# Five regrouped matmuls in place of six for each 128x128 weight tile, in a two-layer trunk on one Trainium2 core

## The chip, the cores and the metric

The kernel runs as one program on one core of a Trainium2 chip. A core has TensorE (PE; its weight loads are shown apart as PEld), VectorE (DVE), ScalarE (ACT), GpSimd (POOL) and SyncE (SP, which issues most DMAs here). The metric is the device time of one execution in microseconds (us): 2583.07 us, the median of three runs (2578.85 to 2583.41).

## The reference

One step of a two-layer model, on a prompt of 512 tokens and 8 samples of one token each. All of it is float32.

```python
for li in range(DEPTH):                                   # DEPTH = 2
    x = x + 0.5 * swiglu(rmsnorm(x, g_ffa), w_gu, w_down)  # 1024 -> 2 x 2816 -> 1024
    if li == 0: m, ... = ab_mixer(rmsnorm(x, g_mix), ...)  # attention + gated delta rule, with a key and value cache
    else:       m, ... = ret_mixer(rmsnorm(x, g_mix), ...) # retention
    x = x + m
    x = x + 0.5 * swiglu(rmsnorm(x, g_ffb), w_gu, w_down)

def swiglu(x, w_gu, w_down):
    a, b = jnp.split(x @ w_gu, 2, axis=-1)
    return (jax.nn.silu(a) * b) @ w_down
```

The attention of the samples (`fox_sample`) also multiplies each sample's query with 2048 cached keys of each of 4 heads: the samples' key scores.

## The kernel before, in words

The 520 tokens (512 + 8) stand in the free dimension, the features in the 128 partitions: X is 8 chunks of 128 features by 520 tokens. Every large product is done the same way. A float32 activation is held as two float32r tiles, high part and rest (XH and XL before a layer, HH and HL inside a feed-forward part, MOH/MOL and RMOH/RMOL behind the mixers), and so is each weight (WHI, WLO). Of the four partial products three are computed: high x high, rest x high weight, high x rest weight. Since a tile of the result has 520 columns and one bank of PSUM holds 512, the tokens are cut into two halves of 260 in two banks (`ACC[acc][:, n, 0:HALF]`). So each 128x128 weight tile costs 3 x 2 = 6 matmuls of 260 columns, and each of these loads its weights anew. That is `project` (L807).

A *unit* is one column block of weights: 8 weight tiles (contraction 1024), or 11 in the down projection, where two units make one tile of the result. For each unit SP loads RAW, POOL makes WHI (L713) and WLO (L716) of it, and PE multiplies; RAW, WHI and WLO have two slots, so POOL starts on unit u+2 when PE is done with unit u (semaphore `used`). The units stand in this order: up0 (44 units), down0 (16), ab_in (29, the first mixer's input projection: one gate unit and 28), ab_out (8), up1, down1, up2, down2, ret_in (48, the second mixer's input), ret_out (16), up3, down3.

The results are taken out by DVE. In `up` a pair of units gives TA (L1815) and TB (L1818), each multiplied by RSTD; ACT applies Silu to TA (L1416), DVE multiplies (TH, L1822), ACT copies TH to HH (L1418), DVE writes HL (L1824). Four accumulators are used in turn. In up0 and down0 the same ACT queue also issues the loads of LF (L1398), four or five behind each step. In `down` DVE adds the result to X (L1799), ACT squares X (SQ) and writes XH, DVE adds SQ to SSQ (L1782) and writes XL (L1784); PE starts on the next `up` chunk by chunk as XL comes. Two accumulators alternate there, as in ab_in.

In ab_in DVE takes each tile out to PRJ (`take`, L1871) and between two takes computes the samples' key scores (`key_scores`, L1882): 32 batches of 16 products of 128 columns, one or two batches behind each of the last 24 takes. The keys come by DMA into KPAGES. Before that stands a serial part on DVE: the gate unit (L1910) and what is computed from it, with the first four takes in between.

The retention's input (ret_in) calls `project` too.

## Time and profile before

| what | us |
|---|---|
| three runs, median (lowest, highest) | 2583.07 (2578.85, 2583.41) |
| span of the profiled execution | 2571.9 |
| so around the span (load and end of the program), by the median | 11.2 |
| PE busy | 2477.0 (96%) |
| DVE, ACT, POOL busy | 1270.5, 565.3, 1680.7 |

The profiled execution has no time of its own beside its span; the median less the span is taken for what lies around it. A line of the page's last sections reads: line, engine, operation, out<-in, shape, count | busy us, mean ns of one | idle us before, and who ended it. A duration of one matmul is longer than the distance from its start to the next one's start, since matmuls are pipelined; so the distance is worked out from a stretch and its count.

### The profile page before, as it was taken

How to read it: one execution, taken by the hardware profiler on the slowest of the kernel's cores; microseconds unless marked ns; L12 is line 12 of the kernel's file. 1: busy time of each engine (PE TensorE's matmuls, PEld its weight loads, DVE VectorE, ACT ScalarE, POOL GpSimd, SP SyncE). 2: the span in 40 equal slices, each digit the busy share in tenths (PEclk: the TensorE clock that was granted, in tenths of full speed). 3: DMA queues.
4: the chain of work that ended last, by engine and by line, in shares of the span. 5: the costliest groups of instructions: out<-in, count | busy, mean ns of one | idle time of the engine just before them, and what ended most of it. 6: DMA issues, size and time to landing. Idle time of an engine off the chain costs nothing.

```text
span 2571.9 us, 52956 instructions
## 1 busy us (share of the span) xinstructions
PE 2477.0 (96%) x20047; PEld 2384.1 (93%) x20047; DVE 1270.5 (49%) x2226; ACT 565.3 (22%) x848; POOL 1680.7 (65%) x750
## 2 busy tenths in 40 slices
PE   7999998998799899999999999999999899999997
PEld 7999998997577899999999999999999799999996
DVE  4444335787533654443344443367767644444433
ACT  3222101004733222220022220012222211222101
POOL 5777775664413477777777777765555367777773
PEclk9999999998899899999999999999999999999998
DMA  4333333895465333333323333233433333333331
GB/s 121 96 93 91 99 90 85 276 317 175 123 213 185 98 88 93 90 96 90 116 83 90 91 95 101 81 93 113 123 101 109 111 90 90 90 91 92 99 95 56
DMA packets 472391, 291.20 MB, mean 113 GB/s; under 512 B 32785, under 2 KB 438411, under 8 KB 472270
## 3 DMA queue, kind: packets, MB, share of 16 engines
q1 hardware_dynamic: 407286, 221.15, 29.6%
q10 hardware_dynamic: 64992, 68.54, 8.4%
q8 instruction: 72, 1.18, 0.2%
q14 instruction: 41, 0.34, 0.0%
HBM read 273.50 MB, written 16.23 MB: 113 GB/s over the span
## 4 chain that ended last, share of the span: by engine, by line
PE 86%; DVE 7%; ACT 3%; POOL 1%; issue 1%; ACTq 1%; DMA 0%; SPq 0%; DVEq 0%; POOLq 0%
PE ACC L807 76%; PE ACC L1075 2%; PE ACC L1044 1%; PE ACC L1317 1%; PE ACC L1327 1%; POOL WLO L716 1%; DVE TB L2318 1%; DVE RMOL L2257 0%; DVE XL L1784 0%; DVE SSR L2235 0%; PE ACC L1329 0%; PE ACC L1142 0%; POOL WHI L713 0%; ACT TAP L1497 0%; PE ACC L901 0%
## 5 line engine op out<-in xcount | busy, mean ns | idle before, releaser
L713 POOL TENSOR_TENSOR WHI<-RAW,ZERO 128x1024 fp32r<-128x1024 f32 (+1 forms) x341 | 691.5, 2028 | 665.0 <-PE ACC L807 625.8
L716 POOL TENSOR_TENSOR WLO<-RAW,WHI 128x1024 fp32r<-128x1024 f32 (+1 forms) x341 | 915.1, 2683 | 49.3 <-POOL WHI L713 2.3
L807 PE MATMUL ACC<-XH,WHI 128*128 128x260 f32 x4032 | 821.6, 285 | 4.2 <-DVE XL L1784 1.9
L807 PE MATMUL ACC<-XH,WLO 128*128 128x260 f32 x4032 | 812.8, 283 | 0.0
L807 PE MATMUL ACC<-XL,WHI 128*128 128x260 f32 x4032 | 811.1, 283 | 0.0
L807 PEld LDWEIGHTS ACC<-XH,WHI 128*128 128x128 f32 x4032 | 624.1, 189 | 22.9 <-DVE PRJ L1871 6.1
L807 PEld LDWEIGHTS ACC<-XH,WLO 128*128 128x128 f32 x4032 | 621.8, 189 | 0.0
L807 PEld LDWEIGHTS ACC<-XL,WHI 128*128 128x128 f32 x4032 | 620.5, 188 | 0.0
L807 PE MATMUL ACC<-HH,WHI 128*128 128x260 f32 x1408 | 284.1, 283 | 1.1 <-POOL WLO L716 1.1
L807 PE MATMUL ACC<-HH,WLO 128*128 128x260 f32 x1408 | 283.1, 282 | 0.0
L807 PE MATMUL ACC<-HL,WHI 128*128 128x260 f32 x1408 | 282.5, 282 | 0.0
L1818 DVE TENSOR_TENSOR TB<-ACC,RSTD 128x520 f32<-128x520 f32 x88 | 61.6, 700 | 420.8 <-PE ACC L807 420.8
L807 PEld LDWEIGHTS ACC<-HH,WHI 128*128 128x128 f32 x1408 | 216.8, 188 | 1.9 <-POOL WLO L716 1.9
L807 PEld LDWEIGHTS ACC<-HL,WHI 128*128 128x128 f32 x1408 | 217.2, 188 | 0.0
L807 PEld LDWEIGHTS ACC<-HH,WLO 128*128 128x128 f32 x1408 | 216.6, 188 | 0.0
L1824 DVE TENSOR_TENSOR HL<-TH,HH 128x520 f32 x88 | 163.5, 1858 | 88.4 <-ACT HH L1418 88.4
L1799 DVE SCALAR_TENSOR_TENSOR X<-ACC,X 128x520 f32 x48 | 33.6, 700 | 349.0 <-PE ACC L807 349.0
L1418 ACT ACTIVATE HH<-TH 128x520 f32 x88 | 56.4, 641 | 541.8 <-DVE TH L1822 541.8
L1822 DVE TENSOR_TENSOR TH<-TA,TB 128x520 f32<-128x520 f32 x88 | 155.2, 1764 | 8.5 <-ACT TA L1416 5.6
L1784 DVE SCALAR_TENSOR_TENSOR XL<-X,PAR,XH x48 | 157.9, 3289 | 0.5
L1388 ACT ACTIVATE SQ<-X 128x520 f32 x48 | 30.8, 641 | 579.3 <-DVE X L1799 579.3
L1416 ACT ACT_TABLE_LOAD x88 | 112.9, 1283 | 97.1 <-issue 95.9
(395 smaller groups left out, 2373.6 us busy)
## 6 DMA issues: line engine op xcount, KB each, us to landing
RAW<-in_ffn_w_gu SPq DMA_DIRECT2D x176, 512.0 KB, 3.8
RAW<-in_ffn_w_down SPq DMA_DIRECT2D x64, 704.0 KB, 4.7
KPAGES<-in_cache_fox_k ACTq DMA_DIRECT2D x128, 256.0 KB, 4.1
RAW<-in_c_w_in SPq DMA_DIRECT2D x48, 512.0 KB, 3.9
VPAGES<-in_cache_fox_v SPq DMA_DIRECT2D x72, 256.0 KB, 3.6
RAW<-in_ab_w_in SPq DMA_DIRECT2D x28, 512.0 KB, 5.7
VPAGES<-in_cache_fox_v ACTq DMA_DIRECT2D x56, 256.0 KB, 3.3
SSR<-in_state_ret_S ACTq DMA_DIRECT2D x8, 1024.0 KB, 6.6
```

Of the source, the lines that this page charges most:

```text
L713: pool.tensor_tensor(WHI[:, slot, 0:nk, :], RAW[:, slot, 0:nk, :], ZERO[:, :].broadcast_to([P, nk, P]), ALU.add).then_inc(hi_split, 1)
L716: pool.tensor_tensor(WLO[:, slot, 0:nk, :], RAW[:, slot, 0:nk, :], WHI[:, slot, 0:nk, :].bitcast(F32), ALU.subtract).then_inc(split, 1)
L807: ins = pe.matmul(ACC[acc][:, n, 0:HALF], w[:, slot, k, :], a[:, k0 + k, n * HALF:(n + 1) * HALF], start=first and opens, stop=final and c ...
L1075: ins = pe.matmul(bank(b)[:, h * P:(h + 1) * P], left(h), right(h), start=start, stop=stop)
L1388: act.activation(SQ[:, :], X[:, bass.ds(d, 1), :].rearrange("p a t -> p (a t)"), ACT.Square).then_inc(sq_ready, 1)
L1416: act.activation(TA[:, :], TA[:, :], ACT.Silu).then_inc(act_ready, 1)
L1418: act.activation(HH[:, bass.ds(j, 1), :].rearrange("p a t -> p (a t)"), TH[:, :], ACT.Copy).then_inc(hh_ready, 1)
L1784: dve.scalar_tensor_tensor(out=XL[:, bass.ds(d, 1), :].rearrange("p a t -> p (a t)"), in0=X[:, bass.ds(d, 1), :].rearrange("p a t -> p (a ...
L1799: dve.scalar_tensor_tensor(out=xd, in0=ACC[s][:, :, 0:HALF], scalar=scale, in1=xd, op0=ALU.mult, op1=ALU.add).then_inc(tile_free, 1)
L1818: dve.tensor_tensor(halves(TB[:, :]), ACC[2 * s + 1][:, :, 0:HALF], halves(RSTD[:, :]), ALU.mult).then_inc(tile_free, 1)
L1822: dve.tensor_tensor(TH[:, :], TA[:, :], TB[:, :], ALU.mult).then_inc(hfull_ready, 1)
L1824: dve.tensor_tensor(HL[:, bass.ds(2 * i + s, 1), :].rearrange("p a t -> p (a t)"), TH[:, :], HH[:, bass.ds(2 * i + s, 1), :].rearrange("p ...
```

## The change

Every product outside ret_in is regrouped. The tokens are cut at 282: LEFT = 282 and RIGHT = 238. High part and rest of an activation stand in one tensor (XS, HS, MOS, RMOS; XH and XL are its halves), so that one matmul can take the right columns of both: 2 x 238 = 476 columns into one bank. That makes five matmuls: 282, 476, 282, 282, 238. What the rest's right columns gave lies beside the right result in the bank (`right_low`) and must be added when the tile is taken out.

```diff
+            def multiply(acc, slot, k, pair, chunk, opens, closes):
+                w_hi, w_lo = WHI[:, slot, k, :], WLO[:, slot, k, :]
+                out_right = ACC[acc][:, 1, 0:2 * RIGHT].rearrange("p (j t) -> p j t", j=2)
+                pe.matmul(left(acc), w_hi, pair[:, 0, chunk, 0:LEFT], start=opens, stop=False)
+                pe.matmul(out_right, w_hi, pair[:, :, chunk, LEFT:TOK], start=opens, stop=False)
+                pe.matmul(left(acc), w_hi, pair[:, 1, chunk, 0:LEFT], start=False, stop=False)
+                pe.matmul(left(acc), w_lo, pair[:, 0, chunk, 0:LEFT], start=False, stop=closes)
+                return pe.matmul(right(acc), w_lo, pair[:, 0, chunk, LEFT:TOK], start=False, stop=closes)
...
-                project(AB_UNIT + f, (AB_UNIT + s) % 2, KD, (s + 1) % 2, XH, XL)
+                project_by_parts(AB_UNIT + f, (AB_UNIT + s) % 2, KD, (s + 1) % 2, XS)
...
 # ACT, in up
+                def copy_lows(tile, acc):
+                    hold(act, used, u0 + tile + 3)
+                    hold(act, lows_added, 2 * KF * f + tile + 1)
+                    act.activation(LOWS[:, acc % 2, :], right_low(acc), ACT.Copy).then_inc(lows_ready, 1)
...
 # DVE, in down
-                        dve.scalar_tensor_tensor(out=xd, in0=ACC[s][:, :, 0:HALF], scalar=scale, in1=xd,
+                        dve.scalar_tensor_tensor(out=xd[:, LEFT:TOK], in0=right(s), scalar=scale, in1=xd[:, LEFT:TOK],
+                                                 op0=ALU.mult, op1=ALU.add).then_inc(right_added, 1)
+                        dve.scalar_tensor_tensor(out=xd[:, 0:LEFT], in0=left(s), scalar=scale, in1=xd[:, 0:LEFT],
+                                                 op0=ALU.mult, op1=ALU.add)
+                        hold(dve, right_added, KD * (r - 1) + d + 1)
+                        dve.scalar_tensor_tensor(out=xd[:, LEFT:TOK], in0=right_low(s), scalar=scale, in1=xd[:, LEFT:TOK],
...
 # DVE, in up
+                def scaled(out, tile, acc):
+                    hold(dve, used, u0 + tile + 3)
+                    dve.tensor_tensor(out[:, 0:LEFT], left(acc), RSTD[:, 0:LEFT], ALU.mult)
+                    hold(dve, lows_ready, 2 * KF * f + tile + 1)
+                    dve.tensor_tensor(right(acc), right(acc), LOWS[:, acc % 2, :], ALU.add).then_inc(lows_added, 1)
+                    hold(dve, lows_added, 2 * KF * f + tile + 3)
+                    dve.tensor_tensor(out[:, LEFT:TOK], right(acc), RSTD[:, LEFT:TOK], ALU.mult).then_inc(tile_free, 1)
...
 # DVE, in ab_in
+            def take_parts(tile, out, acc):
+                dve.wait_ge(used, GATE_UNIT + tile + 3)
+                dve.wait_ge(tile_free, GATE_TILE + tile + 4)
+                dve.tensor_tensor(ABLOW, right_low(acc), RSTD[:, LEFT:TOK], ALU.mult)
+                dve.tensor_tensor(out[:, LEFT:TOK], right(acc), RSTD[:, LEFT:TOK], ALU.mult).then_inc(ab_right, 1)
+                dve.tensor_tensor(out[:, 0:LEFT], left(acc), RSTD[:, 0:LEFT], ALU.mult)
+                dve.wait_ge(ab_right, tile + 1)
+                dve.tensor_tensor(out[:, LEFT:TOK], out[:, LEFT:TOK], ABLOW, ALU.add).then_inc(tile_free, 1)
```

LOWS lies in the tile SQ and ABLOW in SSQ. RGATE, which shared its place with RMOH, now shares it with RMOL.

On PE, two weight tiles of a unit, before and now (the count behind a row is how often it stands in sequence):

```order
L807 MATMUL ACC<-XH,WHI 128x260 x2
L807 MATMUL ACC<-XL,WHI 128x260 x2
L807 MATMUL ACC<-XH,WLO 128x260 x2
L807 MATMUL ACC<-XH,WHI 128x260 x2
L807 MATMUL ACC<-XL,WHI 128x260 x2
L807 MATMUL ACC<-XH,WLO 128x260 x2
```

```order
L816 MATMUL ACC<-XS,WHI 128x282
L817 MATMUL ACC<-XS,WHI 128x476
L818 MATMUL ACC<-XS,WHI 128x282
L819 MATMUL ACC<-XS,WLO 128x282
L820 MATMUL ACC<-XS,WLO 128x238
L816 MATMUL ACC<-XS,WHI 128x282
L817 MATMUL ACC<-XS,WHI 128x476
L818 MATMUL ACC<-XS,WHI 128x282
L819 MATMUL ACC<-XS,WLO 128x282
L820 MATMUL ACC<-XS,WLO 128x238
```

The columns of a weight tile are 1560 in both; its matmuls, and with them its weight loads, are 5 instead of 6.

On DVE in ab_in, from the fourth take on (key scores are the rows with KPAGES), before and now:

```order
L1938 COPY R<-TA 4x8
L1871 TENSOR_TENSOR PRJ<-ACC,RSTD 128x520 x2
L1882 SCALAR_TENSOR_TENSOR KPAGES,SC<-KPAGES,ACC 128x128 x16
L1871 TENSOR_TENSOR PRJ<-ACC,RSTD 128x520
L1882 SCALAR_TENSOR_TENSOR KPAGES,SC<-KPAGES,ACC 128x128 x16
```

```order
L2002 COPY R<-TA 4x8
L1930 TENSOR_TENSOR SSQ<-ACC,RSTD 128x238
L1931 TENSOR_TENSOR PRJ<-ACC,RSTD 128x238
L1932 TENSOR_TENSOR PRJ<-ACC,RSTD 128x282
L1934 TENSOR_TENSOR PRJ<-PRJ,SSQ 128x238
L1930 TENSOR_TENSOR SSQ<-ACC,RSTD 128x238
L1931 TENSOR_TENSOR PRJ<-ACC,RSTD 128x238
L1932 TENSOR_TENSOR PRJ<-ACC,RSTD 128x282
L1934 TENSOR_TENSOR PRJ<-PRJ,SSQ 128x238
L1947 SCALAR_TENSOR_TENSOR KPAGES,SC<-KPAGES,ACC 128x128 x16
```

One operation of 520 columns has become four, the last of them with both inputs in SBUF. The accumulator is free only after the fourth.

## Rows read from the trace of the kernel before

**Rows 1.** The page: busy time, and the granted clock in tenths, 40 slices

```profile
PE 2477.0 (96%) x20047; PEld 2384.1 (93%) x20047; DVE 1270.5 (49%) x2226; ACT 565.3 (22%) x848; POOL 1680.7 (65%) x750
PEclk9999999998899899999999999999999999999998
```

**Rows 2.** Chain that ended last, in time: start us, us, what, count

```profile
34.81 230.66 PE ACC L807 x1920
...
911.11 242.21 PE ACC L807 x2016
1153.39 2.54 POOL WHI L713
1156.10 3.21 POOL WLO L716
1159.34 126.99 PE ACC L807 x1056
```

**Rows 3.** Timeline of PE and PEld, 1697 to 1729: start, us for all, count

```profile
1708.20 1.89 PE L1317 MATMUL ACC<-VTK_R,SQ 128*128 128x256 f32 x8
...
1725.61 0.97 PEld L1343 LDWEIGHTS ACC<-IDENT,READ 128*128 128x128 f32 x8
```

**Rows 4.** Timeline of POOL in up0: start, us, what, idle before

```profile
98.30 1.89 POOL L713 TENSOR_TENSOR WHI<-RAW,ZERO 128x1024 fp32r<-128x1024 f32 x1 [1.04 <-PE ACC L807]
100.34 2.40 POOL L716 TENSOR_TENSOR WLO<-RAW,WHI 128x1024 fp32r<-128x1024 f32 x1
...
106.11 2.69 POOL L716 TENSOR_TENSOR WLO<-RAW,WHI 128x1024 fp32r<-128x1024 f32 x1
```

**Rows 5.** Timelines of DVE and PE where ab_out ends and up1 starts

```profile
904.01 0.70 DVE L1799 SCALAR_TENSOR_TENSOR X<-ACC,X 128x520 f32 x1 [0.59 <-PE ACC L807]
906.41 2.79 DVE L1784 SCALAR_TENSOR_TENSOR XL<-X,PAR,XH  x1
...
909.25 0.50 PE L807 MATMUL ACC<-XH,WHI 128*128 128x260 f32 x2 [0.34 <-DVE XL L1784]
```

**Rows 6.** Timeline of DVE in ab_in: one take and two key scores

```profile
505.64 0.70 DVE L1871 TENSOR_TENSOR PRJ<-ACC,RSTD 128x520 f32<-128x520 f32 x1 [2.75 <-PE ACC L807]
506.26 0.28 DVE L1882 SCALAR_TENSOR_TENSOR KPAGES<-KPAGES,ACC 128x128 f32<-128x128 f32 x1
...
506.46 0.28 DVE L1882 SCALAR_TENSOR_TENSOR KPAGES<-KPAGES,ACC 128x128 f32<-128x128 f32 x1
```

**Rows 7.** Timeline of ACT in up0: one pair of units

```profile
101.59 0.64 ACT L1416 ACTIVATE TA<-TA 128x520 f32<-128x520 f32 x1
106.64 0.64 ACT L1418 ACTIVATE HH<-TH 128x520 f32 x1 [4.41 <-DVE TH L1822]
107.44 3.90 ACTq L1398 DMA_DIRECT2D LF<-in_cache_fox_logf  x4
111.81 1.28 ACT L1416 ACT_TABLE_LOAD   x1 [4.53 <-issue]
```

**Rows 8.** Stretch of ab_in: us, busy PE, PEld, DVE, ACT, POOL; PEclk, DMA, GB/s

```profile
499.50:518.00 18.50, 18.50 (x147) 17.65 (x146) 15.68 (x134) 0.00 (x0) 12.85 (x7) 1.00 0.97 311
```

**Rows 9.** Single lines of DVE, both inputs in SBUF: duration ns min/median/max

```profile
L1822 DVE TENSOR_TENSOR TH<-TA,TB x88: 700/1761/2491, 41.4 to 2418.6; 128x520 f32<-128x520 f32 x88
L2251 DVE TENSOR_TENSOR VBH<-RGATE,VBH x16: 693/698/701, 1741.2 to 2075.5; 128x520 f32<-128x520 f32 x16
```

**Rows 10.** Timeline of DVE ahead of the key scores

```profile
422.27 0.69 DVE L1871 TENSOR_TENSOR PRJ<-ACC,RSTD 128x520 f32<-128x520 f32 x1
425.10 1.42 DVE L1920 TENSOR_SCALAR TH<-TA,COLS 128x520 f32<-128x520 f32 x1 [2.14 <-ACT TB L1452]
...
442.11 0.70 DVE L1871 TENSOR_TENSOR PRJ<-ACC,RSTD 128x520 f32<-128x520 f32 x1
```

**Rows 11.** Waits of PE, 440 to 610: us in total, times, longest

```profile
PE ACC L910 <- DVE PRJ L1871: 6.2, 1, 6.2
```

More of the change, by code:

```diff
@@ L214, in halves, with left, right, right_low @@
             return a.rearrange("p (n t) -> p n t", n=2)
+        LOWS = SQ[:, 0:2 * RIGHT].rearrange("p (j t) -> p j t", j=2)
+        def left(acc):
+            return ACC[acc][:, 0, 0:LEFT]
+        def right(acc):
+            return ACC[acc][:, 1, 0:RIGHT]
+        def right_low(acc):
+            return ACC[acc][:, 1, RIGHT:2 * RIGHT]
         consts_in = sem("consts_in")
@@ L793, in _, with project_by_parts @@
         def _(pe):
+            def multiply(acc, slot, k, pair, chunk, opens, closes):
[6 more added lines that the diff above has]
+                return pe.matmul(right(acc), w_lo, pair[:, 0, chunk, LEFT:TOK], start=False, stop=closes)
+            def project_by_parts(unit, slot, nk, acc, pair, k0=0, last=True, ready=None, late=None):
+                hold(pe, split, unit + 3)
+                for k in range(nk):
+                    if ready is not None:
+                        pe.wait_ge(ready[0], ready[1] + k0 + k)
+                    if late is not None and k0 + k == late[0]:
+                        pe.wait_ge(late[1], late[2])
+                    ins = multiply(acc, slot, k, pair, k0 + k, k == 0 and k0 == 0, last and k == nk - 1)
+                ins.then_inc(used, 1)
             def project(unit, slot, nk, acc, hi, lo, k0=0, last=True, ready=None, late=None):
@@ L845, in load_and_open @@
                     pe.wait_ge(xl_ready, k + 1)
-                    for w, a, opens, closes in ((WHI, XH, True, False), (WHI, XL, False, False), (WLO, XH, False, True)):
-                        for n in range(2):
-                            ins = pe.matmul(ACC[0][:, n, 0:HALF], w[:, 0, k, :], a[:, k, n * HALF:(n + 1) * HALF],
-                                            start=k == 0 and opens, stop=k == KD - 1 and closes)
+                    ins = multiply(0, 0, k, XS, k, k == 0, k == KD - 1)
                 ins.then_inc(used, 1)
-                project(1, 1, KD, 1, XH, XL)
+                project_by_parts(1, 1, KD, 1, XS)
                 pe.wait_ge(tile_free, KD + 4)
                 statistics(0)
-                project(2, 0, KD, 2, XH, XL)
+                project_by_parts(2, 0, KD, 2, XS)
                 pe.wait_ge(std_ready, 1)
-                project(3, 1, KD, 3, XH, XL)
+                project_by_parts(3, 1, KD, 3, XS)
             def up(f, opened=False):
@@ L874, in up, with down @@
                     two_pairs(i)
-            def down(name, hi, lo, nk, per_chunk, ready, late=None):
+            def down(name, pair, nk, per_chunk, ready, late=None):
                 u0, t0 = unit_at[name], tile_at[name]
@@ L882, in down @@
                             n = per_chunk * s + m
-                            project(u0 + 2 * per_chunk * i + n, (u0 + n) % 2, nk, s, hi, lo, k0=nk * m,
-                                    last=m == per_chunk - 1, ready=ready, late=late)
+                            project_by_parts(u0 + 2 * per_chunk * i + n, (u0 + n) % 2, nk, s, pair, k0=nk * m,
+                                             last=m == per_chunk - 1, ready=ready, late=late)
             pe.sem_inc(used, 2)
@@ L1363, in _ @@
                 ret_turn(h, h % 2)
-            down("ret_out", RMOH, RMOL, KD, 2, None, late=(RCH - 2, rm_dve.sem, rm_dve.value("lo1", RET_HEADS - 1)))
+            down("ret_out", RMOS, KD, 2, None, late=(RCH - 2, rm_dve.sem, rm_dve.value("lo1", RET_HEADS - 1)))
             up(3)
-            down("down3", HH, HL, KH, 2, (h_ready, 3 * KF + 1))
+            down("down3", HS, KH, 2, (h_ready, 3 * KF + 1))
             statistics(6)
```

76 lines of the change are left out of this document (40 added, 36 removed).

## The prediction

> **What bounds the kernel now.** I read the page first, then the chain of waits in order of time, then the timelines of single engines at the places where the chain changes its engine. The page shows PE busy for 96% of the span and its clock granted in full except for a few slices [rows 1]. The chain says how: it stays on `project` for hundreds of microseconds, 1920 and 2016 matmuls in a piece through a whole `up` and 1056 through a `down`, and leaves it only for about 6 us of POOL between them and for the mixers [rows 2]. So PE is the bound, and what counts is the distance from one matmul to the next: 242.21 us / 2016 = 120.1 ns, in `down` 126.99 / 1056 = 120.3 ns. A weight tile costs 6 x 120.1 = 720.8 ns.
>
> Is that distance made by columns or by the number of matmuls? 260 columns at the full 2.4 GHz are 108.3 ns, so something else adds 11.8. Two rows bracket it [rows 3]. Eight plain float32 matmuls of 256 columns (L1317; a duration near 0.38 us each) take (1.89 - 0.38) / 7 = 216 ns apart; that is 512 columns' worth at 2.4 GHz (213.3 ns) and 2.6 ns over it. So where the stream is long, nearly nothing is added. Eight matmuls of 4 columns (L1343) load their weights (0.97 - 0.19) / 7 = 111 ns apart: a floor for each matmul with a 128x128 load, whatever its columns. 260 columns of float32r lie beside such a floor. I take 120.1 ns as the floor of a float32r matmul, and stream + 2.6 ns where that is longer.
>
> **The products.** Per weight tile: 282 columns are 117.5 + 2.6 = 120.1 ns, exactly at the floor; 476 are 198.3 + 2.6 = 200.9; 238 are 101.8 and so at the floor, 120.1. Sum 4 x 120.1 + 200.9 = 681.3 ns, 39.5 ns (5.5%) less. The kind of matmul with a 238-column float32r operand is not in the trace, nor one of 282 or 476, so the saving has bounds: if the floor for short ones is L1343's 111 ns, it is 48.5 ns; if the 11.8 ns are a fixed addition to each matmul, it is that one addition, 11.8 ns; if they go with the columns, it is nothing. I take 39.5, since both rows say floor.
>
> Tiles with the new form: up 4 x 44 x 8 = 1408, down 4 x 16 x 11 = 704, ab_out 64, ret_out 128; less 8 in the opening, which wait for X anyway, 2296. ab_in (232 tiles) is treated by itself, ret_in keeps six. 2296 x 39.5 ns = 90.7 us (111 and 27 by the bounds, and 0).
>
> **What can take it back in these stages.** POOL needs 1.89 + 2.69 us and small gaps, 4.9 in all, for a unit in `up` [rows 4]; a unit will last 8 x 0.681 = 5.45 us instead of 5.77, so POOL's idle time shrinks from 1.04 to 0.7 us and stays idle time. Between `up` and `down` it isn't covered: the first unit of `down` needs 2.54 + 3.21 us and gaps [rows 2], about 6, against PE's last unit of 5.77, now 5.45. That is 0.3 us more of waiting, four times: 1.3 us.
>
> Between `down` (or ab_out, ret_out) and the next layer, PE waits for the last XL [rows 5]. The update of X was one operation of 0.70 us. It becomes three; by the pitch of DVE (0.62 us for 520 columns, 0.20 for 128 [rows 6], so about 0.32 for 238 and 0.37 for 282) and a last duration near 0.41 they end after 1.1 us, 0.4 later. PE comes to that chunk 7 x 0.04 = 0.3 us sooner. 0.7 us at five places is 3.5 us with the end of the last `down`.
>
> In `up` DVE gets three operations per tile for one and two round trips to ACT. Per pair it is busy some 6.5 of 10.9 us, and four accumulators give PE three units of slack, so this costs nothing. The tightest place is up0: ACT issues four loads of LF behind each HH, from 106.64 to 111.8 [rows 7], and the two copies of the right lows now stand in the same queue. HH to HH becomes one chain: 5.1 for HH and the loads, 1.28 for a table every other pair or both in one, 0.64 for Silu, two copies (about 0.4), four DVE operations (0.41 and a wait each), TH 1.76: 11 to 11.5 us per pair against PE's 10.9. Over 22 pairs that is up to 10 us of lag, which the accumulators and the late use of the last chunks absorb. I take 0, at worst 5.
>
> **ab_in, where the sign turns.** In a stretch of three units, 18.5 us, DVE is busy 15.68 [rows 8] and waits 2.75 for PE [rows 6]. So PE is the bound here, but narrowly. A take costs DVE 0.62 us of queue now. The four operations cost 0.32 + 0.32 + 0.37, and the last one 0.41 if POOL is idle. That one has both inputs in SBUF, and such operations are slow beside POOL: TH takes 700 ns at least and 1761 at the median, while the same kind in ret_in, with POOL idle, takes 698 [rows 9]. Scaled to 238 columns, 0.89. POOL starts on new weights just when a unit ends, that is when the take is made. So a take costs 1.42 to 1.9 us; I take 1.75, that is 1.13 more. Per three units DVE then needs 15.68 + 3 x 1.13 = 19.1 us, more than PE's 3 x 5.45 and a broadcast of 1.05: 17.4. The bound moves to DVE, and the period goes from 18.5 to 19.1 (18.1 to 19.5). Eight periods: 4.6 us lost (3.5 gained to 8 lost) where the matmuls alone would have given 9.2. DMA, at a share of 0.97 [rows 8], would not have let it gain all of that either.
>
> The Trainium skill ("SBUF — State Buffer", its rules on the shared port pair) says that a DVE instruction with two SBUF inputs contends with a GpSimd instruction that reads SBUF, and one with a single SBUF input doesn't. The trace agrees: 698 against 1761 ns [rows 9], and 0.70 for the take from PSUM while POOL works [rows 6]. It speaks against this change, as the added last operation is of the slow kind; by the rule every take beside POOL costs 1.9.
>
> Ahead of the key scores DVE is the chain: from 425.10 on it works without a pause to the fourth take at 442.11 [rows 10], and PE waits 6.2 us for that [rows 11]. The gate's take and three more stand on it (one, at 422.27, is followed by 2.14 us of idle time and is covered): 4 x 1.13 = 4.5 us. PE idles longer there, and its clock has a slice at 8 near it [rows 1]; another microsecond for that.
>
> **Sum.** 90.7 - 1.3 - 3.5 - 4.5 - 1.0 - 4.6 = 75.8 us. The span was 2571.9 and the median of the runs 2583.1; what lies around the span, 11.2 us, isn't touched. 2583.1 - 75.8 = 2507 us.
>
> **Rivals.**
> *Fixed addition.* Each matmul has its 11.8 ns beyond its columns. For it: 120.1 is over both 111 and 110.9. Against it: L1317's 2.6 ns. The gain is 27 us less the same 15 of costs: 2571.
> *Low floor.* Short matmuls come down to 111 ns, and the takes mostly miss POOL: 111 - 5.8 - 4 + 3.5 = 105 us, 2478. For it: L1343. Against it: 260 columns never went below about 120 on the mean.
> *Slower: TensorE pays by the column.* A float32r column costs 120.1 / 260 = 0.462 ns on the way from SBUF, and the number of matmuls nothing. Then 1560 columns cost 720.8 ns as before, and what remains is DVE's and ACT's new work, some 15 us: 2598. It decides as soon as a tile gains less than 15 / 2296 = 6.5 ns. Against it: no row of float32r with another width can be set against the 260. For it: the same lack, and that plain float32, which streams twice, shows no such addition.
> *Only DVE counts more than I think:* up0 held by ACT's loads and takes of 1.9 throughout, 10 us more: 2517, within the range.
>
> The Trainium skill ("TensorE: Matmul & The Clock Gate", back-to-back issue gap and LDWEIGHTS) gives N / 2.4 + 2.5 ns, and 107 ns for a load of 128 columns. By these figures a tile goes from 6 x 110.8 = 665 to 3 x 120.0 + 200.8 + 106.7 = 667.5 ns, an estimate of no gain, and the time would be that of the slower rival. The trace doesn't agree on the start of it: it has 120.1 ns at 260 columns [rows 2], not 110.8.
>
> **Chances.** The forecast with its own range of 2495 to 2522 (the added DVE work from half to twice) 0.68; low floor 0.13; fixed addition 0.07; the slower rival 0.09; something else, such as a wait between ACT and DVE that holds `up`, 0.03. From the 2478 of the low floor up to 2560, which leaves out the slower rival and the fixed addition, is 0.8. A difference of 0.2%, about 5 us, is what a measurement can tell from no change: faster 0.87, same 0.03, slower 0.10.
>
> **What the profile afterwards would show.** In the chain, pieces of `up` with 1680 matmuls and a mean distance of 136 ns (681 / 5), 229 us instead of 242; 709 / 5 = 142 would be the fixed addition, 144 payment by the column, and below 134 the low floor. In ab_in, DVE without idle time before a take and PE waiting for PRJ; if PE stays the bound there, my take is too dear. POOL's waits for PE shorter, about 0.7 us, in `up`. In the gate's part PE's wait of 6.2 us grown to 11 or 12. I am wrong in kind, not in size, if the distance in `up` is 144 ns, or if PE waits for TA or TB's tiles in `up`.

## The result, and the profile after

The changed kernel takes 2597.4 us (median of four runs, 2589.3 to 2598.6) where the kernel before, measured beside it, took 2583.2 (four runs, 2578.9 to 2586.5). The ratio is 1.0059, 95% interval 1.0043 to 1.0075: 0.6% slower. Forecast were 2507 us and a range of 2478 to 2560, with 0.10 for slower. The time is that of the slower rival, "TensorE pays by the column", which had given 2598; how much of that agreement is luck is said further down.

The profiled execution has a span of 2587.5 us against 2571.9, 15.6 more. The page of the changed kernel: busy time and clock [rows 1], then the groups of its costliest instructions (line, engine, operation, operands, shape, count | busy us, mean ns of one | idle before and its releaser). L816 to L820 are the five matmuls of a weight tile.

```profile
PE 2481.4 (96%) x17511; PEld 2315.2 (89%) x17511; DVE 1353.3 (52%) x2761; ACT 627.8 (24%) x1024; POOL 1673.6 (65%) x750
PEclk9999998998899899999999999999999999999998
L817 PE MATMUL ACC<-XS,WHI 128*128 128x476 f32 x1640 | 628.0, 383 | 0.0
L816 PE MATMUL ACC<-XS,WHI 128*128 128x282 f32 x1640 | 488.3, 298 | 11.6 <-DVE PRJ L1934 5.6
L820 PE MATMUL ACC<-XS,WLO 128*128 128x238 f32 x1640 | 452.4, 276 | 0.0
```

PE has 2536 matmuls fewer and is as busy as before. The weight loads (PEld) fell from 93% to 89% of the span, and yet PE is not done sooner. DVE has 83 us more to do.

The same per stage, from the last matmul of one stage to the last of the next, in us:

| stage | before | after | difference |
|---|---|---|---|
| opening and up0 | 276.70 | 275.86 | -0.84 |
| down0 to down3, each | 127.25 | 127.84 | +0.6, four times |
| gate's unit and four more | 32.43 | 34.86 | +2.4 |
| 24 units of ab_in beside the key scores | 160.36 | 170.31 | +9.95 |
| first mixer, ab_out | 306.82 | 307.38 | +0.6 |
| up1 to up3, each | 255.23 | 255.09 | -0.14, three times |
| ret_in | 400.26 | 401.70 | +1.4 |
| ret_out and the tail | 120.56 | 120.73 | +0.2 |

Each column of this table is one profiled execution. Two rows vary by themselves: in the experiments below whose code there is that of the kernel before, "first mixer, ab_out" took 303.7 to 310.8 us and ret_in 400.3 to 403.4, so their +0.6 and +1.4 are no effect that can be told from none.

So next to nothing came from 2296 regrouped tiles. A unit of eight tiles in `up` takes 5.753 us instead of 5.767: 719.1 ns per tile for 720.9. A tile in `down` takes 723.4 ns for 720.0; why it is dearer there than in `up` stays open.

The timeline of PE inside one unit of the changed kernel (start us, us of one, line) shows where a tile's time goes:

```profile
547.35 0.29 PE L816 MATMUL ACC<-XS,WHI 128*128 128x282 f32 x1
547.48 0.38 PE L817 MATMUL ACC<-XS,WHI 128*128 128x476 f32 x1
547.70 0.29 PE L818 MATMUL ACC<-XS,WHI 128*128 128x282 f32 x1
547.83 0.29 PE L819 MATMUL ACC<-XS,WLO 128*128 128x282 f32 x1
547.96 0.28 PE L820 MATMUL ACC<-XS,WLO 128*128 128x238 f32 x1
```

From start to start that is 0.13, 0.22, 0.13, 0.13 us. Over all such pairs of up0 the means are 132 ns behind L816, 219 behind L817, 128 and 129 behind L818 and L819, and 112 behind L820. The forecast had 120.1, 200.9 and again 120.1 for the three widths. The short one did go below 120, the long ones cost more than forecast.

The loss is where the key scores are. The stretch of ab_in that answers to [rows 8], a little longer (busy us of PE, PEld, DVE, ACT, POOL; granted clock, DMA share, GB/s):

```profile
500.00:540.00 40.00, 38.81 (x245) 35.44 (x246) 39.79 (x287) 0.00 (x0) 25.79 (x13) 0.96 0.90 290
```

DVE was busy 15.68 of 18.5 us [rows 8] and is now busy 39.79 of 40. It has become the bound, as the forecast said. Three units take 19.96 us instead of 18.54 (the pattern now repeats after six units, 39.92 us). The timeline of DVE, one take and the last operation of two others (against [rows 6]):

```profile
523.74 0.41 DVE L1930 TENSOR_TENSOR SSQ<-ACC,RSTD 128x238 f32<-128x238 f32 x1
524.06 0.40 DVE L1931 TENSOR_TENSOR PRJ<-ACC,RSTD 128x238 f32<-128x238 f32 x1
524.38 0.44 DVE L1932 TENSOR_TENSOR PRJ<-ACC,RSTD 128x282 f32<-128x282 f32 x1
524.73 1.29 DVE L1934 TENSOR_TENSOR PRJ<-PRJ,SSQ 128x238 f32<-128x238 f32 x1
...
530.49 2.57 DVE L1934 TENSOR_TENSOR PRJ<-PRJ,SSQ 128x238 f32<-128x238 f32 x1
...
540.85 1.17 DVE L1934 TENSOR_TENSOR PRJ<-PRJ,SSQ 128x238 f32<-128x238 f32 x1
```

The same operation takes 1.29, 2.57 and 1.17 us here. Its line's own view gives minimum, median and maximum in ns:

```profile
L1934 DVE TENSOR_TENSOR PRJ<-PRJ,SSQ x28: 395/1172/2633, 423.9 to 610.4; 128x238 f32<-128x238 f32 x28
```

What stands around the take of 540.85 on PE and POOL, from the timeline of all engines:

```profile
539.77 1.12 PE L937 MATMUL ACC<-TH,IDENT 8*128 8x512 f32 x2
539.87 1.89 POOL L731 TENSOR_TENSOR WHI<-RAW,ZERO 128x1024 fp32r<-128x1024 f32 x1 [1.32 <-PE ACC L820]
...
542.08 0.40 PE L816 MATMUL ACC<-XS,WHI 128*128 128x282 f32 x1 [1.19 <-DVE PRJ L1934]
```

POOL starts on the next weights at 539.87, when the unit ends, and is done at 541.76. The add that starts at 540.85 ends at 542.02, 0.26 us behind POOL, and PE, which waits for that accumulator, starts at 542.08 after 1.19 us of idle time. The slowest of the three adds shown above started 0.09 us behind this POOL instruction, which runs until 532.79:

```profile
530.40 2.39 POOL L734 TENSOR_TENSOR WLO<-RAW,WHI 128x1024 fp32r<-128x1024 f32 x1
```

It ended at 533.06, 0.27 us later. So it is with all of them: 22 of the 29 adds (the gate's among them) start while a POOL instruction runs, and each of the 22 ends 0.262 to 0.272 us behind the end of that instruction; the seven that meet none take 0.395 to 0.398 us. The add is held until POOL's instruction ends, and what it costs is what is left of that instruction. The trace of the kernel before shows the same for TH (L1822, [rows 9]): 87 of 88 end 0.555 to 0.558 us behind the POOL instruction that they met.

Behind the wait of 1.19 us the granted clock falls. The stretch from 543.6 to 547.0 us shows

```profile
543.60:547.00 3.40, 3.40 (x15) 3.19 (x14) 3.37 (x24) 0.00 (x0) 0.70 (x1) 0.50 0.86 275
```

that is 1.2 GHz, with 15 matmuls where 23 stand in the 3.0 us behind. There are three such stretches in this stage (from 502.6, 543.6 and 601.6 us), and none in the kernel before between 449.7 and 613.5 us. That they cost little here is argued and not measured: DVE, the bound, is busy 3.37 of the 3.40 us all the same.

Ahead of the key scores PE's waits (us in total, times, longest), against the 6.2 of [rows 11]:

```profile
PE ACC L946 <- DVE PRJ L1934: 4.9, 1, 4.9
...
PE ACC L816 <- DVE TA L1934: 2.3, 1, 2.3
PE ACC L968 <- DVE PRJ L1934: 1.7, 1, 1.7
```

The last two are not new: the same waits were 1.0 (for TA) and 0.8 us (L932) in the kernel before. The 4.9 us lie behind the four units, at the start of the stage with the key scores. What the gate's part lost is at the wait for TA, here after and before:

```profile
419.73 0.40 PE L816 MATMUL ACC<-XS,WHI 128*128 128x282 f32 x1 [2.29 <-DVE TA L1934]
...
418.24 0.51 PE L807 MATMUL ACC<-XH,WHI 128*128 128x260 f32 x2 [0.96 <-DVE TA L1910]
```

Behind the longer wait the clock falls, where the kernel before has it in full:

```profile
420.70:424.10 3.40, 3.40 (x15) 3.20 (x14) 3.37 (x6) 1.10 (x2) 1.23 (x1) 0.50 0.27 72
...
420.70:424.10 3.40, 3.40 (x31) 3.40 (x30) 2.25 (x2) 1.71 (x2) 1.09 (x1) 1.00 0.31 73
```

From its first matmul to its last that unit takes 7.34 us instead of 5.73. So of the 2.4 us, 1.3 are the wait and 1.6 the clock, and a wait of 0.6 us two units later is gone.

The chain in time answers to [rows 2]. It shows the last XS (which stands where XL stood), the statistics (L855), and POOL between `up` and `down` with the same 2.54 and 3.2 us as before:

```profile
921.55 0.76 DVE XS L1830
922.35 0.40 PE ACC L816
923.33 0.88 PE ACC L855 x4
1165.98 2.54 POOL WHI L731
1168.68 3.20 POOL WLO L734
```

Between 924.21, where the statistics end, and 1165.98 lie the same 336 tiles as in [rows 2] (2016 / 6). 241.77 us over 1680 matmuls are 143.9 ns from one to the next; the forecast's list had 144 for payment by the column and 136 for its own case.

### The profile page after: what moved, and what is told of

It reads as the page before. It is cut to its first block, busy times and chain, and to the rows that moved or that the text cites. A ratio compares the mean times of both kernels' runs of the same rounds, so it can differ in the third digit from the quotient of the medians.

```text
span 2587.5 us, 49474 instructions
## 1 busy us (share of the span) xinstructions
PE 2481.4 (96%) x17511; PEld 2315.2 (89%) x17511; DVE 1353.3 (52%) x2761; ACT 627.8 (24%) x1024; POOL 1673.6 (65%) x750
## 4 chain that ended last, share of the span: by engine, by line
PE 66%; DVE 12%; ACT 3%; issue 2%; POOL 1%; ACTq 1%; DMA 0%; DVEq 0%; POOLq 0%
PE ACC L817 15%; PE ACC L816 9%; PE ACC L818 9%; PE ACC L819 9%; PE ACC L820 8%; PE ACC L846 7%; DVE KPAGES L1947 3%; PE ACC L1111 2%; DVE PRJ L1934 1%; PE ACC L1080 1%; DVE TB L2382 1%; PE ACC L1353 1%; PE ACC L1363 1%; DVE RMOS L2321 1%; DVE SSR L2299 1%
## 5 line engine op out<-in xcount | busy, mean ns | idle before, releaser
L817 PE MATMUL ACC<-XS,WHI 128*128 128x476 f32 x1640 | 628.0, 383 | 0.0
L816 PE MATMUL ACC<-XS,WHI 128*128 128x282 f32 x1640 | 488.3, 298 | 11.6 <-DVE PRJ L1934 5.6
L819 PE MATMUL ACC<-XS,WLO 128*128 128x282 f32 x1640 | 479.4, 292 | 0.0
L818 PE MATMUL ACC<-XS,WHI 128*128 128x282 f32 x1640 | 478.3, 292 | 0.0
L820 PE MATMUL ACC<-XS,WLO 128*128 128x238 f32 x1640 | 452.4, 276 | 0.0
L819 PEld LDWEIGHTS ACC<-XS,WLO 128*128 128x128 f32 x1640 | 309.6, 189 | 48.0
L816 PEld LDWEIGHTS ACC<-XS,WHI 128*128 128x128 f32 x1640 | 314.0, 191 | 20.4 <-DVE PRJ L1934 8.3
L818 PEld LDWEIGHTS ACC<-XS,WHI 128*128 128x128 f32 x1640 | 314.4, 192 | 0.0
L817 PEld LDWEIGHTS ACC<-XS,WHI 128*128 128x128 f32 x1640 | 313.7, 191 | 0.4 <-issue 0.2
L820 PEld LDWEIGHTS ACC<-XS,WLO 128*128 128x128 f32 x1640 | 311.9, 190 | 0.0
L817 PE MATMUL ACC<-HS,WHI 128*128 128x476 f32 x704 | 268.9, 382 | 0.0
L846 PE MATMUL ACC<-XS,WHI 128*128 128x260 f32 x1536 | 253.2, 287 | 1.5 <-DVE XS L1830 0.7
L846 PEld LDWEIGHTS ACC<-XS,WHI 128*128 128x128 f32 x1536 | 212.1, 188 | 11.3 <-DVE VBH L2273 5.5
L816 PE MATMUL ACC<-HS,WHI 128*128 128x282 f32 x704 | 207.3, 294 | 1.1 <-POOL WLO L734 1.1
L819 PE MATMUL ACC<-HS,WLO 128*128 128x282 f32 x704 | 205.8, 292 | 0.0
L818 PE MATMUL ACC<-HS,WHI 128*128 128x282 f32 x704 | 205.8, 292 | 0.0
L820 PE MATMUL ACC<-HS,WLO 128*128 128x238 f32 x704 | 193.8, 275 | 0.0
```

The source lines that it names most:

```text
L816: pe.matmul(left(acc), w_hi, pair[:, 0, chunk, 0:LEFT], start=opens, stop=False)
L817: pe.matmul(out_right, w_hi, pair[:, :, chunk, LEFT:TOK], start=opens, stop=False)
L818: pe.matmul(left(acc), w_hi, pair[:, 1, chunk, 0:LEFT], start=False, stop=False)
L819: pe.matmul(left(acc), w_lo, pair[:, 0, chunk, 0:LEFT], start=False, stop=closes)
L820: return pe.matmul(right(acc), w_lo, pair[:, 0, chunk, LEFT:TOK], start=False, stop=closes)
L846: ins = pe.matmul(ACC[acc][:, n, 0:HALF], w[:, slot, k, :], a[:, k0 + k, n * HALF:(n + 1) * HALF], start=first and opens, stop=final and c ...
```

## Experiments on the price of a matmul

First question: is 120.1 ns a floor, an addition or the price of 260 columns? Five kernels change the width, the kind or the place of the moving operand in the `up` stages of the kernel before. Each was run once, and what it computes is no longer the reference's; the price is read inside its stages. Each `up` stage has its own value, and one unit (48 matmuls) gives the distance.

**Wide.** In `project`, for the `up` stages, with MODE = (300, 400, 500, 512) columns by stage:

```diff
+ if mode and (k > 0 or mode > HALF):
+     at = 0 if n == 0 else TOK - mode
+     out, moving = ACC[acc][:, n, 0:mode], a[:, k0 + k, at:at + mode]
```

> The kernel before, with wider matmuls in the four up stages: 300, 400, 500 and 512 columns in place of 260 (both matmuls of a pair read overlapping tokens, so columns are computed twice and the output is another one). Theory C, TensorE pays 0.461 ns for each float32r column: distances of 138, 185, 231 and 236 ns in up0, up1, up2, up3. Rival F, the theory of the prediction (a floor of 120 ns, and columns at 2.4 GHz plus 2.6 ns above it): 128, 169, 211 and 216 ns.

Measured: units of 6.593, 8.727, 10.867 and 11.123 us, so 137.4, 181.8, 226.4 and 231.7 ns per matmul. Windows inside the four stages (us, PE busy with its count first) give the same, as 400 / 1768 = 226:

```profile
200.00:300.00 100.00, 100.00 (x730) 100.00 (x729) 37.38 (x30) 19.48 (x24) 67.39 (x31) 1.00 0.30 81
1000.00:1300.00 300.00, 300.00 (x1652) 299.96 (x1651) 84.14 (x68) 43.56 (x51) 150.83 (x68) 1.00 0.21 61
1500.00:1900.00 400.00, 400.00 (x1768) 331.90 (x1767) 90.38 (x73) 46.80 (x55) 163.82 (x74) 1.00 0.17 49
2600.00:3000.00 400.00, 400.00 (x1727) 324.00 (x1727) 89.64 (x72) 46.08 (x54) 159.66 (x72) 1.00 0.16 47
```

The four lie on one line, 4.0 ns + 0.4448 ns per column, and at 260 columns it gives 119.7. So a float32r column costs 0.4448 ns at a granted clock of 1.00, and not 1 / 2.4 = 0.4167. Theory C had the right form at 0.461. Of the 11.8 ns that the forecast took for a floor, 260 x 0.028 = 7.3 go with the columns and 4.0 with the matmul. The floor theory is out.

**Narrow.** The same edit with MODE = (250, 240, 200, 128), for all tiles of a unit but its first.

> The kernel before, with narrower matmuls in the four up stages: 250, 240, 200 and 128 columns in place of 260, behind each unit's first weight tile (the other columns of the products are left out). Theory C, 0.461 ns per column and the 111 to 112 ns of a weight load as a floor: 115, 112, 112, 112 ns. Rival F, a floor of 120 ns for every float32r matmul: 120 in all four, and the time of the kernel before. By C the time falls by 2112 matmuls a stage x (5 + 8 + 8 + 8 ns) = 61 us.

Measured: units of 5.607, 5.433, 5.400 and 5.400 us. Less the first tile (0.721 us) and over 42 matmuls: 116.3, 112.2, 111.4, 111.4 ns. There is a floor, and it is that of the weight loads in [rows 3], 111 ns: at 250 columns the line still holds nearly (115.2), at 240 the floor does.

```profile
200.00:250.00 50.00, 50.00 (x431) 50.00 (x430) 20.62 (x17) 12.16 (x14) 39.73 (x18) 1.00 0.35 95
...
1300.00:1500.00 200.00, 200.00 (x1780) 200.00 (x1780) 91.49 (x74) 47.32 (x56) 163.71 (x75) 1.00 0.33 97
```

PEld is busy for the whole window here, and for 324 of 400 us at 512 columns. In the kernel before it was busy for 93%: 260 columns lie just above the floor, by 8 or 9 ns, and narrower matmuls can gain no more than that each. A regrouping keeps the 1560 columns; by the line it can only save the 4.0 ns of each matmul that it leaves out, and four matmuls, the fewest that 512 columns allow, would save 8 ns of a tile. Both are estimates from the line.

**Kinds.** 260 columns, but up0 moves one column repeated (stride 0), up1 one zero repeated, up2 the high halves of all numbers as bf16 (every second of 520), and up3 that with 500 columns:

```diff
+ if mode == "stride0" and k > 0:
+     moving = a[:, k0 + k, 0:1].broadcast_to([P, HALF])
...
+ if mode in ("half", "half500") and k > 0:
+     weights = weights.bitcast(BF16)[:, 1::2]
+     moving = moving.bitcast(BF16)[:, 1::2]
```

> The kernel before, with another moving operand in the up stages behind each unit's first weight tile (the products are others): up0 reads one column again and again (stride 0), up1 reads zeros (one element again and again), up2 reads weights and activations as bfloat16 (the upper half of each float32, every second element), up3 the same with 500 columns. What makes a column dearer than 1 / 2.4 GHz? If the float32r format itself does: 120, 120, 111 and 211 ns. If the data do (power): up1 alone falls to 111. If fetching new addresses from SBUF does: up0 and up1 fall to 111, and up2 stays at 120.

Measured: units of 5.433, 5.476, 5.613 and 10.653 us, so 112, 113, 116.5 and 221 ns.

```profile
200.00:250.00 50.00, 50.00 (x445) 50.00 (x444) 23.15 (x19) 11.15 (x14) 40.47 (x20) 1.00 0.36 99
950.00:1130.00 180.00, 180.00 (x1580) 180.00 (x1579) 81.19 (x67) 43.45 (x51) 143.97 (x66) 1.00 0.33 96
1300.00:1500.00 200.00, 200.00 (x1713) 170.43 (x1711) 87.90 (x72) 45.46 (x54) 156.50 (x72) 1.00 0.32 93
```

A repeated column is at the floor although it is as many columns, float32r, and not zero. So at 260 columns the excess over the floor depends on what is read for the moving operand, not on how many columns are multiplied. The bf16 halves fit none of the three expectations (111 and 211, or 120): 116.5 and 221 ns are 4.0 and 0.43 ns per column.

**Fetch.** Again 260 columns in each stage, with: up0 weights repeated, moving as before; up1 four columns repeated; up2 every second column; up3 130 columns read twice.

```diff
+ if mode == "weight0" and k > 0:
+     weights = w[:, slot, k, 0:1].broadcast_to([P, P])
+ if mode == "four" and k > 0:
+     moving = a[:, k0 + k, 0:4][:, None, :].broadcast_to([P, HALF // 4, 4])
+ if mode == "stride2" and k > 0:
+     moving = a[:, k0 + k, n:TOK:2]
+ if mode == "twice" and k > 0:
+     moving = a[:, k0 + k, 0:HALF // 2][:, None, :].broadcast_to([P, 2, HALF // 2])
```

> The kernel before; in its up stages every matmul behind the first weight tile of a unit has 260 columns, but in up0 its weights are one column repeated (stride 0), in up1 its moving columns are 4 columns repeated, in up2 every second column of the operand, in up3 130 columns each read twice. What it computes there is no longer the reference's. Theory 1 (a column costs 0.445 ns because the moving operand is fetched element by element, and only a repeated single element is free of that): unit of up0 5.77 us (weights don't matter), up2 and up3 5.77 us, up1 5.77 us if each repeat is fetched anew. Theory 2 (the extra time over the 111 to 112 ns floor is moving and weight fetches in each other's way): up0 5.43 us, with the others 5.77 us. Theory 3 (fetching few distinct places is cheap): up1 5.43 us, up3 between.

Measured: units of 5.653, 5.433, 10.483 and 5.893 us, so 117.4, 112.2, 232.4 and 123.1 ns.

```profile
200.00:260.00 60.00, 60.00 (x512) 60.00 (x511) 25.05 (x21) 14.73 (x17) 47.63 (x22) 1.00 0.35 96
950.00:1140.00 190.00, 190.00 (x1681) 190.00 (x1680) 87.20 (x72) 45.40 (x53) 153.13 (x71) 1.00 0.33 98
1300.00:1700.00 400.00, 400.00 (x1833) 360.07 (x1832) 94.29 (x76) 48.63 (x57) 168.35 (x76) 1.00 0.17 51
```

Theory 2 (weight reads in the way) explains 2.7 of the 8 to 9 ns at most, theory 3 (few places are cheap) holds for four columns. Reading 130 columns twice is no cheaper than 260 neighbours, but 3 ns dearer. The doubling at stride 2 had been in nobody's expectation: 260 columns cost what 512 neighbours do.

**Room.** Is it the width that the operand spans? up0 has 10 columns repeated 26 times, up1 20 repeated 13 times, up2 130 columns out of 260 (stride 2), up3 130 out of 520 (stride 4).

```diff
+ if mode in ("r10", "r20") and k > 0:
+     m = int(mode[1:])
+     moving = a[:, k0 + k, 0:m][:, None, :].broadcast_to([P, HALF // m, m])
+ if mode == "s2" and k > 0:
+     out, moving = ACC[acc][:, n, 0:130], a[:, k0 + k, 0:HALF:2]
+ if mode == "s4" and k > 0:
+     out, moving = ACC[acc][:, n, 0:130], a[:, k0 + k, 0:TOK:4]
```

> The kernel before; in its up stages, behind the first weight tile of a unit, the moving operand is: in up0 10 columns repeated 26 times and in up1 20 columns repeated 13 times (260 columns each), in up2 130 columns taken as every second of 260, in up3 130 columns taken as every fourth of 520. What it computes there is no longer the reference's. Theory 1, the width of SBUF that the moving operand spans sets the time (every second column of 520 took 232 ns, as 520 neighbouring ones would): up2 5.77 us per unit (120 ns as for 260 neighbouring columns), up3 about 10.5 us (232 ns) at one rate for every stride. Theory 2, the number of columns sets it and stride 2 only doubled each: up2 5.77 us too, but up3 no more than up2. Theory 3, a column costs only when it is not in the piece fetched before: up0 and up1 lie between 5.43 us (floor, as with 4 columns repeated) and 5.89 us (as 130 columns read twice); if 10 columns still fit into one piece up0 5.43 us.

Measured: 5.470, 5.860, 5.700 and 5.760 us, so 113.1, 122.4, 118.6 and 120.0 ns.

```profile
1310.00:1520.00 210.00, 210.00 (x1771) 210.00 (x1770) 90.91 (x74) 46.85 (x56) 162.59 (x75) 1.00 0.32 92
2200.00:2400.00 200.00, 200.00 (x1669) 200.00 (x1668) 85.71 (x70) 43.47 (x51) 151.89 (x70) 1.00 0.31 92
```

Theory 1 is out (stride 4 would be 232). A column at stride 2 costs 0.88 ns, twice that of a neighbour: 4.0 + 130 x 0.88 = 118.4 and 4.0 + 260 x 0.88 = 232.8. Ten repeated columns are nearly at the floor and twenty are not, which theory 3 allows. It doesn't say why twenty repeated cost 122.4 ns, more than 260 neighbours. What is read at once, and why a neighbour costs 0.4448 ns, stays open.

**Six.** Now the other side of the change. The changed kernel with its matmul of 476 columns cut into two of 238, so six per tile again, with the same columns:

```diff
- pe.matmul(out_right, w_hi, pair[:, :, chunk, LEFT:TOK], start=opens, stop=False)
+ for j in range(2):
+     pe.matmul(out_right[:, j], w_hi, pair[:, j, chunk, LEFT:TOK], start=opens and j == 0, stop=False)
```

> The changed kernel, with the 476-column matmul cut into two of 238 again: six matmuls and six weight loads per tile, 1560 columns as before. Theory C: the two of 238 are at the load's 112 ns each, 224 in place of 219, so a tile costs 726 in place of 722 ns and the kernel 2528 x 5 ns = 12 us more than the changed one. Rival F (a matmul costs at least 120 ns): 240 in place of 201, 2528 x 39 ns = 100 us more.

Measured: one run of 2619.3 us, 47 over the kernel before on its chip (2572.2), where the changed kernel is 14 over. A unit of `up` takes 5.880 us, 735 ns per tile, 15.9 more than with five. The expectation of payment by the column was 5 more, that of the floor 39. It is nearer to the first, and 11 ns stay unexplained by the line: six matmuls of 282 and 238 columns cost 735 where six of 260 cost 721. From start to start the means in up1 show where they are: the two of 238 take 225.0 ns where the one of 476 took 219.2, as expected, but the two of 282 behind them take 132.5 and 134.0 instead of 127.7 and 128.6. Why, no run shows. The line plus the floor at 238 columns gives 3 x 129.4 + 215.7 + 111.4 = 715 ns for the changed tile; measured are 719.

**Cut at 264 and 256.** If 238 columns lie at the floor, 256 waste nothing. The changed kernel with LEFT = 264, so matmuls of 264, 512, 264, 264 and 256 columns, of the same sum:

```diff
- LEFT = 282
+ LEFT = 264
```

> The changed kernel with the tokens cut at 264 and 256 in place of 282 and 238: matmuls of 264, 512, 264, 264, 256 columns. Theory C with the line that the two width runs gave, 4.0 ns + 0.4448 ns per column and 112 ns at least: 3 x 121.4 + 231.7 + 117.9 = 713.9 ns per tile against 716 by the same line for the changed kernel (its units show 719 in up, 723 in down), so 5 to 12 us less than the changed kernel. Rival F: no tile gains, and the time is within 2 us of the changed kernel.

Measured: ratio to the kernel before 1.0027 (1.0015 to 1.0040), against 1.0059 (1.0043 to 1.0075) for the changed kernel. A tile takes 715.0 ns in `up` and 715.5 in `down` (713.9 by the line). That is what one matmul less and no floor are worth, 5.9 ns of 721. It is 0.3%, about 8 us, less than the changed kernel, as theory C had it (5 to 12); rival F is out. ab_in is as slow as in the changed kernel (171.2 us).

```profile
100.00:260.00 160.00, 160.00 (x1121) 149.83 (x1120) 92.33 (x113) 45.03 (x70) 123.68 (x57) 1.00 0.34 92
```

**Corrections as bf16.** In the kernel before, the two correction products (XL by WHI and XH by WLO) read the high halves of both operands as bf16:

```diff
+ weights, moving = w[:, slot, k, :], a[:, k0 + k, n * HALF:(n + 1) * HALF]
+ if not opens:
+     weights, moving = weights.bitcast(BF16)[:, 1::2], moving.bitcast(BF16)[:, 1::2]
```

> The kernel before, with the two correction products of each tile (rest x high weight, high x rest weight) multiplied as bfloat16: the upper half of each float32 word, every second element, nothing copied. The products differ in their last bits only. From the run with bfloat16 in up2 (unit of 5.613 us, so 116.5 ns at 260 columns against 120.1): 4 x 3.6 = 14.4 ns per tile and 2912 tiles, 42 us less than the kernel before, 2541. Rival: the change between formats from one matmul to the next costs as much as it gives, and the time is that of the kernel before.

Measured: ratio 0.9970 (0.9958 to 0.9982), about 8 us less and not 42. A tile takes 716.6 ns. From start to start the means in up0 are 121.4 ns from the second float32r matmul to the first of XL by WHI, 130.2 to the second of them, then 115.7 and 115.9 for XH by WLO, and 233.3 for the last step back to float32r and the next one together. Sum 716.5, where two matmuls of 120.1 and four of 116.5 would give 706.2. The loss lies in the second step, from the first bf16 matmul to the second: 130.2 ns, 13.7 more than 116.5. The step back to float32r costs nothing that can be seen (233.3 for 116.5 + 120.1). So 10 of the 14.4 ns that bf16 should save are given back behind the change to bf16. The rival was right in kind, but not that nothing is left.

## Experiments on the takes

**Input projection as before.** The changed kernel, but ab_in and the gate's unit with `project` and one take of 520 columns:

```diff
- project_by_parts(AB_UNIT + f, (AB_UNIT + s) % 2, KD, (s + 1) % 2, XS)
+ project(AB_UNIT + f, (AB_UNIT + s) % 2, KD, (s + 1) % 2, XH, XL)
...
- take_parts(f + 1, PRJ[:, f, :], (s + 1) % 2)
+ hold(dve, used, AB_UNIT + f + 3)
+ dve.tensor_tensor(PRJ[:, bass.ds(f, 1), :].rearrange("p a (n t) -> p (a n) t", n=2),
+                   ACC[(s + 1) % 2][:, :, 0:HALF], halves(RSTD[:, :]), ALU.mult).then_inc(tile_free, 1)
```

> The changed kernel with ab_in as it was (six matmuls of 260, one operation per take), the rest regrouped. Theory 1, the loss is DVE's work in ab_in and ahead of it, since the matmuls gain and lose nothing elsewhere: ab_in back from 170.3 to 160.4 us, the gate's part from 34.9 to 32.4, and 12 to 13 us less than the changed kernel, 1 to 4 us over the kernel before. Rival 2, the loss is spread over the regrouped stages (X's three operations, copies on ACT, pairs in up): at least 10 us over the kernel before remain.

Measured: ratio 1.0011 (1.0000 to 1.0021), ab_in 161.6 us and the gate's part 32.8. Of the 12.4 us lost there, 10.7 are back, as theory 1 had it. What is left over the kernel before, 2.8 us by the ratio, is of the size of what the four `down` lose (4 x 0.6).

```profile
500.00:540.00 40.00, 40.00 (x310) 37.32 (x309) 34.51 (x293) 0.00 (x0) 27.70 (x13) 1.00 0.96 311
```

**A take without two SBUF inputs.** Is it the number of operations, or the last one's kind? Again four operations, but the addition is made in PSUM, so that none has both inputs in SBUF. The first one copies the low part, the last one multiplies (some of its lines):

```diff
- dve.tensor_tensor(ABLOW, right_low(acc), RSTD[:, LEFT:TOK], ALU.mult)
...
- dve.tensor_tensor(out[:, LEFT:TOK], out[:, LEFT:TOK], ABLOW, ALU.add).then_inc(tile_free, 1)
+ dve.tensor_copy(ABLOW, right_low(acc)).then_inc(ab_right, 1)
...
+ dve.tensor_tensor(right(acc), right(acc), ABLOW, ALU.add).then_inc(ab_right, 1)
...
+ dve.tensor_tensor(out[:, LEFT:TOK], right(acc), RSTD[:, LEFT:TOK], ALU.mult).then_inc(tile_free, 1)
```

> The changed kernel with another take in ab_in, also of four operations, but none with two inputs in SBUF: right_low is copied to SBUF, added to the right part inside PSUM, and that is multiplied by RSTD. Theory 1a, the last operation of the take is dear because it stands against POOL's weight splitting (395 to 2633 ns for 238 columns): a take falls to 1.5 us, DVE needs 15.7 + 3 x 0.9 = 18.4 us per three units, PE 18.5, and ab_in comes back to 161 to 163 us, 8 to 9 us less than the changed kernel. Rival 1b, four operations and their waits are dear as such: ab_in stays over 168 us.

Measured: ratio 1.0035 (1.0022 to 1.0047), ab_in 162.95 us, the gate's part 34.2. The addition's own row, and the window of ab_in:

```profile
L1933 DVE TENSOR_TENSOR ACC<-ACC,SSQ x29: 398/404/404, 418.4 to 602.0; 128x238 f32<-128x238 f32 x29
```

```profile
500.00:540.00 40.00, 40.00 (x260) 35.87 (x259) 39.12 (x315) 0.00 (x0) 27.48 (x13) 1.00 0.97 308
```

The addition takes 404 ns at most instead of up to 2633, and PE is never idle in the window, with its clock in full. So of the 9.95 us lost in ab_in, 7.4 are one kind of operation beside POOL, with the falls of the clock that came behind it (this run has none from 452.1 us to the end of ab_in), and 2.6 the rest; that this is the four operations and their waits in place of one is argued, not tested by itself. DVE is still busy 39.12 of 40 us: no room is left. In the gate's part it gives back only 0.6 of 2.4 us: the clock stays in full there, but PE waits 1.8 us for TA and 1.2 at the unit where the changed kernel has no wait.

**Both together.** The changed kernel with LEFT = 264 and the input projection as before:

> The changed kernel with the cut at 264 and 256 columns, and the input projection of the first mixer with its gate unit as in the kernel before (six matmuls per tile, one take). From the units of the earlier runs: up stages 5.720 instead of 5.767 us per unit, 1.6 us less in each of four; down stages 7.870 instead of 7.920, 0.75 us less in each of four; output projections about 1.0 us less together; the gate part and input projection about 1.6 us more and the second mixer's input projection about 1.5 us more, as the run with the old input projection showed at 282 and 238. Sum about 8 us less than the kernel before, ratio 0.997. If the new cut's gain is eaten at the stage edges, ratio 1.000.

Measured: 2570.6 us against 2578.0, ratio 0.9971 (0.9957 to 0.9986). `up` 253.63 us, `down` 126.50, ab_in 161.3, all as expected from the parts. It beats both kernels, and the one before by 7.4 us where 8 had been expected; it is level with the bf16 corrections.

```profile
100.00:260.00 160.00, 160.00 (x1121) 149.83 (x1120) 92.29 (x113) 45.03 (x70) 123.70 (x57) 1.00 0.34 92
```

## Why the prediction was wrong

- **The step that failed: "I take 120.1 ns as the floor of a float32r matmul, and stream + 2.6 ns where that is longer".** 120.1 ns is the price of 260 columns, 4.0 + 260 x 0.4448 = 119.7, and the floor is at 111.4. The term of 90.7 us was about 1 us in up0, nothing over the later `up` stages and less than nothing in `down` (-0.6 each). The tile that was to take 681.3 ns takes 719.1.
- **Why it looked sound.** One row was plain float32, 216 ns for 256 columns, read as "512 columns' worth at 2.4 GHz". That column rate was carried to float32r, and 120.1 then left 11.8 ns to explain. The wide runs show that the rate doesn't carry over: 226.4 ns for 500 float32r columns. The other row, 111 ns, was right and was the floor; the forecast set it aside as the lesser bound. The forecast also noted that no row had float32r at another width, and gave the rival that this leaves open 0.09. Two rows of other kinds had been taken for a measurement of this kind. The bound "nothing" was in the text, and the range left it out.
- **ab_in: right in kind, mis-sized.** DVE became the bound there, as said. A take costs 2.00 us of DVE's queue (from its first operation to the next instruction behind it, mean of the six that repeat), 1.38 more than before, where 1.13 was taken: 15.68 + 3 x 1.38 = 19.8 us, and the period is 19.96. The last operation is 1.08 on the mean and not 0.89, since it isn't slowed by a factor: it is held until POOL's instruction ends and then takes 0.26 us. Scaling 1761 ns by the columns was the error. Forecast 4.6 us lost, measured 9.95; the stretch between the fourth unit and the first of the 24 is 1.3 us shorter than before, so the 24 units themselves lost 11.3.
- **The gate's part: 4.5 us forecast (and one for the clock), 2.4 measured, of which the clock is 1.6.** The wait of 6.2 us did not grow to 11 or 12, it fell to 4.9: DVE ends the fourth take only 0.9 us later (443.71 for 442.81), and PE comes 2.2 us later to it. The chain on DVE was no sum of fixed times: in the kernel before TH (L1922) took 2.78 us there beside POOL, and the same operation takes 0.70 in the changed kernel, where it meets none.
- **The edges of stages: forecast 1.3 + 3.5 us.** 44 units of `up` at 14 ns less make -0.6 us, and the stage shows -0.14, so the edge costs about 0.45 us where 0.7 was taken. In `down` 16 units at 37 ns more make +0.59 of +0.6. POOL's 2.54 + 3.20 us between them are as before, but a unit of `up` isn't shorter, so this term is zero.
- **In `up` nothing waits on DVE or ACT**, as forecast at 0, with 83 us more work on DVE in the whole kernel.
- **That 2598 was so near is luck in part.** The rival was right that the matmuls gain nothing. Its 15 us of costs were the forecast's 1.3 + 3.5 + 4.5 + 1.0 + 4.6; measured are 12.4 in ab_in and the gate's part where 10.1 were taken, and at the edges nothing for the 1.3 and about two thirds of the 3.5; the `down` stages lost 2.4 that nobody had counted. Its price was not the measured one either: 0.462 ns per column and nothing for a matmul, where the runs show 0.4448 and 4.0, and a floor.
- **Around the span: 11.2 us were taken, 1.8 lie there** (the run of 2589.3 us has a span of 2587.5). The rest is that the profiled execution of the kernel before, 2571.9 us, was quicker than its four timed runs. This moved nothing in the forecast, which only took a difference from the median.
- **The page's rule.** By the figures in the Trainium skill ("TensorE: Matmul & The Clock Gate", back-to-back issue gap) the tile gained nothing, 665 against 667.5 ns, and the forecast turned this down because the row of 120.1 didn't agree with 110.8. The sizes are indeed not those (719.1 and 720.9), and the trace has 0.4448 ns per column and 4.0 for each matmul, but the form, a small addition to each matmul and the rest by the column, was the right one. The section calls that formula the gap of an isolated matmul, and gives about 131 ns for 512 columns in a stream of loads and matmuls; the trace doesn't agree, it has 231.7 there (the wide run). A rule that is off by 8% at one point can still have the right form.
